# Two transformer blocks on one core: the 256 best keys of query tiles 5 to 7 found by bisection instead of by rounds of eight maxima

## The reference

```python
logits = jnp.einsum('bthd,bsd->bths', qib, k_idx) * (IDX_DIM ** -0.5)
score = jnp.einsum('bth,bths->bts', wb, jax.nn.relu(logits))
score = jnp.where(causal[None], score, -jnp.inf)
_, sel = lax.top_k(score, topk)            # topk = 256
sel_ok = sel <= tb[None, :, None]
k_sel, v_sel = k[sel], v[sel]              # gathered per query
s = jnp.einsum('btkgd,btnkd->btkgn', qg, k_sel) * (HEAD_DIM ** -0.5)
p = jax.nn.softmax(jnp.where(sel_ok, s, -jnp.inf), axis=-1)
o = jnp.einsum('btkgn,btnkd->btkgd', p, v_sel)
```

## Time and profile before

| | |
|---|---|
| median of 3 runs | 2946.56 us (2946.21 to 2955.95) |
| the profiled execution, its own time | 2957.97 us |
| its span, first to last instruction | 2956.2 us |
| mean granted clock of TensorE | 0.97 of full speed |
| busy: PE, DVE, ACT, POOL | 93%, 60%, 23%, 40% of the span |

### The profile page before, as it was taken

How to read it: one execution, slowest core, us unless ns; L and a number is a source line. 1 busy time by engine, 2 the same in 40 slices (tenths; PEclk the granted TensorE clock), 3 DMA queues, 4 the chain that set the end, 5 groups by cost and what they waited for, 6 DMA issues and landing times.

```text
span 2956.2 us, 34504 instructions
## 1 busy us (share of the span) xinstructions
PE 2758.8 (93%) x13488; PEld 2277.8 (77%) x13488; DVE 1763.9 (60%) x2232; ACT 681.4 (23%) x1154; POOL 1196.3 (40%) x791
## 2 busy tenths in 40 slices
PE   4988988999999999999999999788889999999998
PEld 4867766778778888888886768677778888888887
DVE  6288999985566566567566784355535344444335
ACT  4231223443231111000113342122214000111002
POOL 2421476544454344344332323333344344344332
PEclk8999999989999999999999999899999999999999
DMA  6201011110321111111112110000031111111111
GB/s 212 65 12 32 22 58 58 51 43 22 128 72 43 43 57 50 38 54 57 40 50 93 43 36 29 1 1 1 29 129 58 49 57 43 43 57 50 38 54 57
DMA packets 142487, 153.32 MB, mean 52 GB/s; under 512 B 7183, under 2 KB 105252, under 8 KB 142374
## 3 DMA queue, kind: packets, MB, share of 16 engines
q1 hardware_dynamic: 136512, 141.87, 15.2%
q10 hardware_dynamic: 5862, 9.89, 0.9%
HBM read 143.35 MB, written 8.39 MB: 51 GB/s over the span
## 4 chain that ended last, share of the span: by engine, by line
PE 79%; DVE 15%; issue 2%; ACT 2%; POOL 1%; DMA 1%; ACTq 0%; SPq 0%; DVEq 0%; POOLq 0%
PE ps L1813 11%; PE ps L1814 11%; PE ps L1815 11%; PE ps L1798 10%; PE ps L1800 10%; PE ps L1799 10%; PE ps L2200 3%; DVE score L1344 3%; DVE best L1342 3%; DVE yt L1635 2%; PE ps L1972 1%; DVE yt L1624 1%; DVE score L1358 1%; PE ps L1962 1%; PE ps L1998 1%
## 5 line engine op out<-in xcount | busy, mean ns | idle before, releaser
L1798 PE MATMUL ps<-h_hi,w_hi 128*128 128x512 f32 x1472 | 585.3, 398 | 10.3 <-issue 5.6
L1799 PE MATMUL ps<-h_lo,w_hi 128*128 128x512 f32 x1472 | 575.4, 391 | 0.0
L1800 PE MATMUL ps<-h_hi,w_lo 128*128 128x512 f32 x1472 | 575.3, 391 | 0.0
L669 POOL TENSOR_TENSOR w_hi<-raw,zero 128x1024 fp32r<-128x1024 f32 x128 | 243.7, 1904 | 780.3 <-PE ps L1800 397.3
L1813 PE MATMUL ps<-w_hi,u_hi 128*128 128x512 f32 x1024 | 399.2, 390 | 0.0
L1814 PE MATMUL ps<-w_lo,u_hi 128*128 128x512 f32 x1024 | 398.9, 390 | 0.0
L1815 PE MATMUL ps<-w_hi,u_lo 128*128 128x512 f32 x1024 | 398.8, 389 | 0.0
L1519 DVE TENSOR_TENSOR act_r<-act_r 128x512 f32<-128x512 f32 x128 | 167.5, 1309 | 328.9 <-ACT act_r L1035 328.7
L672 POOL TENSOR_TENSOR w_lo<-raw,w_hi 128x1024 fp32r<-128x1024 f32 x128 | 338.1, 2642 | 10.1
L1798 PEld LDWEIGHTS ps<-h_hi,w_hi 128*128 128x128 f32 x1472 | 278.0, 189 | 78.1 <-issue 17.5
L1035 ACT ACTIVATE act_r<-ps 128x512 f32<-128x512 f32 x128 | 76.4, 597 | 1130.8 <-PE ps L1800 1130.8
(11 more groups left out here) (380 smaller groups left out, 4348.4 us busy)
## 6 DMA issues: line engine op xcount, KB each, us to landing
raw<-in_w_up_dram SPq DMA_DIRECT2D x64, 512.0 KB, 4.0
raw<-in_w_down_dram SPq DMA_DIRECT2D x64, 512.0 KB, 3.2
raw<-in_w_ada_dram SPq DMA_DIRECT2D x48, 512.0 KB, 3.7
raw<-in_w_in_dram SPq DMA_DIRECT2D x32, 512.0 KB, 3.7
raw<-in_w_out_dram SPq DMA_DIRECT2D x32, 512.0 KB, 3.2
x<-in_x_dram SPq DMA_DIRECT2D x8, 512.0 KB, 10.8
x<-in_x_dram ACTq DMA_DIRECT2D x8, 512.0 KB, 7.9
x_mid<-x SPq DMA_DIRECT2D x8, 512.0 KB, 5.4
```

The source lines that it names most:

```text
L669: g_.tensor_tensor(w_hi[:, r, :], raw[:, r, :], zero.to_broadcast([P, 1024]), ALU.add).then_inc(sem("w_hi_done"), 1)
L1798: mm(ps[:, bank, :], wh, h_hi[:, k, cols], start=(k == 0), stop=False)
L1799: mm(ps[:, bank, :], wh, h_lo[:, k, cols], start=False, stop=False)
L1800: last = mm(ps[:, bank, :], wl, h_hi[:, k, cols], start=False, stop=(k == NK - 1))
```

## The change

The rounds of tiles 5, 6 and 7 (`SEL_TILES`) are gone. In their place a threshold is found for each of the 3 * 128 queries by bisection over the bits of a float: 1 pass for the sign of the 256th score, 8 for its exponent, 23 for its mantissa, 32 passes (`SEL_PASSES`).

- `sel_pass(k)`, on ACT: three activations, one for each tile (768, 896 and 1024 wide). Each computes the sign of (scale * score + candidate) and sums it along the row into one number. Each waits for the one before it, and pass k waits for step k - 1.
- `sel_step(k)`, on DVE: waits for the three sums, then four linked instructions on 128 x 3 elements accept or refuse the candidates and make the next ones (step 8 has five, the last ten).
- `sel_fin(t, part)`, on DVE: six parts for each tile that correct the last bit, count the keys above the threshold, number the ties by a running sum, keep as many as are wanted, and write the mask.

Passes 0 to 9 stand on ACT between the last scores and the copies `pr_q`; their steps stand on DVE after every third of the rounds 24 to 50, step 9 ahead of the rotation of the queries. Passes 10 to 31 lie in slots 0 to 21, each step in the next slot behind the row maximum. The rounds of tile 4 are spread over slots 0 to 23, and the finishing parts over slots 23 to 29, 32 to 40 and 43 to 48. GpSimd gets five small memsets.

```diff
+SEL_TILES = IDX_TILES[3:]
+NSEL = len(SEL_TILES)
+EXPONENTS = (127, 63, 32, 16, 8, 4, 2, 1)
+SEL_PASSES = 1 + len(EXPONENTS) + 23
...
-        TOPK_SLOTS = {4: range(0, 7), 5: range(7, 20), 6: range(20, 36), 7: range(36, 54)}
+        TOPK_SLOTS = {4: range(0, 24)}
+        SEL_EARLY, SEL_ROUNDS = 10, 3
+        SEL_AT = {k - SEL_EARLY: k for k in range(SEL_EARLY, SEL_PASSES)}
+        FIN_SLOTS = {}
+        for ti, at_slots in zip(SEL_TILES, ((23, 24, 25, 27, 28, 29), (32, 33, 35, 36, 38, 40), (43, 44, 45, 46, 47, 48))):
+            for part, n in enumerate(at_slots):
+                FIN_SLOTS[n] = ("sel_fin", ti, part)
...
                 MICRO.append(("scores", t, i))
+                if n - 1 in SEL_AT:
+                    MICRO.append(("sel_step", SEL_AT[n - 1], 0))
...
+                if n in FIN_SLOTS:
+                    MICRO.append(FIN_SLOTS[n])
+                if n in SEL_AT:
+                    MICRO.append(("sel_pass", SEL_AT[n], 0))
                 if n in ADA_SLOTS:
                     MICRO.append(("ada", ADA_SLOTS[n], 0))
...
+            def sel_pass(k, out):
+                for e, t in enumerate(SEL_TILES):
+                    n = NSEL * k + e
+                    if k == 0:
+                        act.wait_ge(sem("acc_done"), len(INDEX))
+                    else:
+                        act.wait_ge(sem("sel_cand"), k)
+                    if n:
+                        act.wait_ge(sem("sel_sum"), n)
+                    s.activation(out[:, 0:(t + 1) * P], score[t], ACT.Sign, scale=sel_t["sign"][:, e:e + 1] if k else -1.0,
+                                 bias=sel_t["cand"][:, e:e + 1] if k else zero,
+                                 accum_out=sel_t["sum"][:, e:e + 1]).then_inc(sem("sel_sum"), 1)
...
+            for k in range(SEL_EARLY):
+                sel_pass(k, sel_early)
             for t in range(NT):
                 act.wait_ge(sem("tm_full"), 2 * NT + t + 1)
...
+            def sel_step(k):
+                d = sel_t
+                dve.wait_ge(sem("sel_sum"), NSEL * (k + 1))
...
+                link(v.tensor_tensor(d["acc"], d["sum"], d["rank"], ALU.is_le))
+                link(v.tensor_tensor(d["pick"], d["acc"], d["cand"], ALU.mult))
+                link(v.tensor_tensor(d["low"], d["low"], d["pick"], ALU.max))
+                done = len(EXPONENTS)
+                if k < done:
+                    v.tensor_scalar(d["cand"], d["low"], 2.0 ** EXPONENTS[k], None, ALU.mult).then_inc(sem("sel_cand"), 1)
...
+                elif k < SEL_PASSES - 1:
+                    v.scalar_tensor_tensor(d["cand"], d["base"], 2.0 ** (done - 1 - k), d["low"], ALU.mult,
+                                           ALU.add).then_inc(sem("sel_cand"), 1)
...
+            def sel_fin(t, part):
+                e, sc, w = t - SEL_TILES[0], score[t], (t + 1) * P
...
+                junk = sel_out[:, 0:w]
+                if part == 0:
+                    link(v.tensor_scalar(junk, sc, d["sign"], d["pick"], ALU.mult, ALU.is_lt))
+                    link(v.tensor_reduce(d["above"], junk, AX.X, ALU.add))
...
+                if part == 2:
+                    link(v.tensor_scalar(junk, sc, d["kth"], None, ALU.is_gt))
+                    link(v.tensor_reduce(d["higher"], junk, AX.X, ALU.add))
+                    link(v.tensor_scalar(d["ties"], d["higher"], -1.0, float(TOPK), ALU.mult, ALU.add))
+                if part == 3:
+                    link(v.tensor_scalar(junk, sc, d["kth"], None, ALU.is_equal))
+                    link(v.tensor_tensor_scan(junk, ones[:, 0:1].to_broadcast([P, w]), junk, 0.0, ALU.mult, ALU.add))
+                if part == 4:
+                    link(v.tensor_scalar(junk, junk, d["ties"], None, ALU.is_le))
+                    link(v.scalar_tensor_tensor(junk, sc, d["kth"], junk, ALU.is_equal, ALU.mult))
+                if part == 5:
+                    link(v.scalar_tensor_tensor(sc, sc, d["kth"], junk, ALU.is_gt, ALU.add))
+                    link(v.tensor_scalar(sc, sc, 0.0, MASKED, ALU.is_equal, ALU.mult))
...
-            for t, r in ROUND[EARLY_ROUNDS:TOPK_Q]:
+            for n, (t, r) in enumerate(ROUND[EARLY_ROUNDS:TOPK_Q]):
                 topk(t, r)
+                if n % SEL_ROUNDS == SEL_ROUNDS - 1 and n // SEL_ROUNDS < SEL_EARLY:
+                    sel_step(n // SEL_ROUNDS)
```

More of the change, by code:

```diff
@@ L155, in build @@
         alog = small("alog", [P, GH])
+        sel_t = {nm: at(f"sel_{nm}", [P, NSEL], F32, off[0] + 32 * i)
+                 for i, nm in enumerate(("wide", "sum", "rank", "sign", "low", "base", "cand", "acc", "pick", "value", "next",
+                                         "step", "many"))}
+        sel_s = {nm: at(f"sel_{nm}", [P, 1], F32, off[0] + 32 * (13 + i))
+                 for i, nm in enumerate(("above", "is_next", "exact", "kth", "higher", "ties"))}
         abraw = small("abraw", [P, NK, 2 * GH])
@@ L1424, in _ @@
                     topk(t, i)
+                if kind == "sel_step":
+                    sel_step(t)
+                if kind == "sel_fin":
+                    sel_fin(t, i)
                 if kind == "divide":
```

39 lines of the change are left out of this document (added).

## The result

The kernel after takes 2960.84 us (median of 20 runs, 2955.99 to 2964.51), the kernel before 2951.61 us (median of 20 runs beside them, 2946.21 to 2960.27); the ratio is 1.003, with a 95% interval of 1.0021 to 1.0038. That is within the 0.5% that I called no difference, but on the side that I had not forecast: I had said 2940.3.

A forecast was written before the change was run, and what follows sets the result against it. The prediction took PE as the bound over the whole execution and DVE in slots 0 to 47. Its terms, 9.5 + 9 - 24.5 = -6 us, gave 2940.3 us against the median of 2946.6; range 2908 to 2970.

The forecast's parts named there:

- The bound: Attention stage: DVE bounds slots 0 to 21 and 22 to 47 only; slots 48 to 63 gain nothing.
- The early passes, +9.5: Before the attention stage: passes and steps delay the copy of `pr_q` and the queries' rotation; +9.5 us, ends +4 and +14.
- A pass of 3.85 us: ACT: three activations of 1.14 us, each with 0.14 us of waiting for the sum before, 3.85 us a pass.
- A step of 2.3 us: DVE, slots 0 to 21: 0.84 us for four linked instructions plus 1.4 meetings with GpSimd instructions, 2.3 us.
- Slots 0 to 21, +9: First stretch: pass, step and 0.1 us make a slot of 6.25 us, 137.5 us in all; +9, ends -9 and +68.
- That wait is covered, as long as a slot lasts over 5 us: DVE, slots 0 to 21: the next row maximum, done some 8 us after this slot's exponential, is wanted after 12.
- Slots 22 to 47, -24.5: Second stretch: rounds gone, PE needs 143 us, DVE some 102; 153.5 us taken, -24.5, ends -32 and -12.
- The sum: Whole kernel: 9.5 + 9 - 24.5 = -6 us, 2940.3 against the median of 2946.6.
- The loop as the new bound: Rival, slots 0 to 21: steps of 3.45 us, slots of 7.4, stretch +34, sum +19, 2966 us; chance 0.22.
- Steps that run free: Rival: GpSimd mostly idle when steps begin; slots 0 to 21 take 120 us, sum -27, 2920 us; chance 0.30.
- The second stretch that doesn't shrink: Rival, slots 22 to 47: `sel_fin` and GpSimd block each other, only 10 us won, sum +8, 2955 us; chance 0.08.
- ACT is busy for less than 80% of slots 0 to 21 and the stretch is still longer than now: Slots 0 to 21: one of the signs named in advance that would show the forecast wrong.

The follow-up runs named there:

- the pass last: The kernel after with only the order within a slot changed, ScalarE's pass behind the product and the copy of its slot; 2957.22 us, ratio to before 1.0016.
- the kernel without passes: The kernel after with the bisection ended after eleven passes, passes 11 to 31 and their steps left out; 2924.19 us, ratio to before 0.9905.
- the kernel without the loop: The kernel after with attention-stage passes that read a constant column, write unread sums and wait for no step; 2944.60 us, ratio to before 0.9969.
- pointer steps: The kernel after with each step done tile by tile on one column, other operands as per-partition scalars; 2940.26 us, ratio to before 0.9960.
- pointer steps and the pass last: The kernel after with one-column pointer steps in the attention stage, queries' copy after pass 7, and the pass last in its slot; 2930.94 us, ratio 0.9929.
- the shorter execution of the kernel before: Third profiled execution of the unchanged kernel before; 2950.26 us, slots 22 to 47 in 175.11 us.
- The last step alone: The kernel after with only the seven added operations of pass 31's step done tile by tile on one column with pointers; 2957.43 us, ratio to before 1.0010.
- 131.2 in another: The kernel after with four-operation early steps, queries' copy after pass 7, and one-column pointer steps in the attention stage; 2938.73 us, ratio to before 0.9945.

## Why the prediction was wrong

**The bound, right.** DVE held up slots 0 to 47 and nothing behind them: slots 48 to 63 take 101.75 us in every kernel here.

**The early passes, +9.5: right**, though the first profiles of the two kernels seemed to say +6.5. Counted from the last gate copy, which neither kernel moves, they cost 9.5. The mechanism was the one described (passes of 3.9 us, 54.98 us from pass 0 to the copy of `pr_q`, PE idle for 7.4 us where I had said about 5), and moving the copy gives 6.5 of it back.

**A pass of 3.85 us: right**, 3.87 (activations of 1.03, 1.14 and 1.24 us and what stands between them).

**A step of 2.3 us: right** in the mean, 2.13. (The prediction's 1.05 us for the mean GpSimd instruction is 1.10 by its own counts, which would make the step 2.4.)

**Slots 0 to 21, +9: wrong, +16.3 to 16.6.** The step that failed is "a slot of 3.85 + 2.3 + 0.1 = 6.25", and with it "That wait is covered, as long as a slot lasts over 5 us". The sum lets a step begin when its pass ends. From the start of the first pass of the stretch to that of the last there are 140.1 us: 81.1 are the 21 passes, 44.8 the 21 steps, and 13.1 are time in which the pass had ended and the step had not begun, because VectorE was not through with the row maximum that stands ahead of it; 1.1 are left. The sum has nothing for the 13.1. Of these, 12.5 lie in a few places: 2.76 and 2.90 us in the second slots of tiles 1 and 2, 2.94 behind the pass of slot 20, 1.79, 0.92, 0.86 and 0.36 behind four others.

In the second slots of tiles 1 and 2 the attention output of the tile before is split. There VectorE's row maximum stands behind `h_lo`, which waits for `h_hi`, which stands on ScalarE behind the pass and the product. The timeline of ACT and DVE at the first of them:

```profile
417.92 1.24 ACT L950 ACTIVATE sel_out<-score,sel_cand,sel_sign 128x1024 f32<-128x1024 f32 x1
...
419.16 1.13 ACT L1018 ACTIVATE raw<-raw,csil 128x1024 f32<-128x1024 f32 x1
...
420.20 0.57 ACT L1023 ACTIVATE h_hi<-ps 128x512 fp32r<-128x512 f32 x1
...
420.88 0.69 DVE L1553 TENSOR_TENSOR h_lo<-ps,h_hi 128x512 fp32r<-128x512 f32 x1 [3.74 <-ACT h_hi L1023]
```

The exponential then came at 422.13, 8.97 us behind the one before (7.28 us in the kernel before, 6.60 with the pass last). In the kernel with the pass last the late beginnings fall from 13.1 to 2.4 us, but the steps grow by 3.0, and ScalarE, with the product now behind the exponential, is itself late by 3.2 us more, and the first pass begins 1.0 later; 3.7 us of the stretch are won.

In the other places the row maximum waited for PE's scores. Behind the pass of slot 20, PE had waited for GpSimd's diagonal and then worked at the lower level, 0.62 us for a matmul of a tap in place of 0.39:

```profile
489.23 0.56 PE L2115 MATMUL ps<-glu_hi,diag_hi 128*128 128x504 f32 x1 [2.08 <-POOL diag_lo L678]
...
494.56 0.56 DVE L1527 CUSTOM_DVE_ANT_0 prob<-ps,score 128x384 f32<-128x384 f32 x1 [4.38 <-issue]
```

(The profile names no releaser for the second line; PE's last matmul of these scores ends at 494.43.) That slot takes 8.04 us, and 9.13 in the kernel without passes, so this is not the work of the passes. Two more slots are over 8 us, those of 8.24 and 8.06: they hold the two longest steps of the stretch, 4.32 and 4.33 us. PE's waits of 9.4 us for the convolution's bank, behind the copy at L1030, are 6.9 us in the kernel without the loop, 9.0 with pointer steps, and 9.5 with pointer steps and the pass last, so little of the loop's 18.8 us can be theirs. The prediction asked who waits behind the step on DVE, and didn't ask who waits behind the pass on ACT, or whether the step could begin when the pass ended.

**Slots 22 to 47, -24.5: wrong, -19.3** (and -16.6 against the shorter execution of the kernel before). The 153.5 us forecast for this stretch are what it takes when the last step is out of the way (153.20, and 152.79 with pointers); with it, it is 158.5. The step that failed is one that isn't there: the prediction costed "four linked instructions" for every step, though the section on the change says that the last one has ten, seven of them each behind a GpSimd instruction, with slot 23's row maximum behind them. It is the meeting that I had priced, on the longest chain of them, at a place that I didn't ask about. The last step alone is worth 3.8 us; the other 1.2 of the 5 us were not followed.

**The sum.** It was -6 and came to +9. Of the 15 us between, 7.5 are slots 0 to 21, 5 are slots 22 to 47 against the first profile, and 2.7 are in that profile itself, whose second stretch was 177.79 where the third had 175.11. The remaining 5 us between 2940.3 and 2960.8 are the median of the kernel before, 2946.6 of three runs and 2951.6 of twenty.

**The rivals.** The loop as the new bound had the right mechanism and the wrong lever: it asked for steps of 3.45 us, and with steps of 2.13 the kernel was already slower. Steps that run free is what the pointer form makes true: 126.4 us where the rival said 120. There, too, steps begin late, by 9.4 us in all, and neither the rival nor the forecast has that term. The second stretch that doesn't shrink is false. Of the marks in the prediction, "ACT is busy for less than 80% of slots 0 to 21 and the stretch is still longer than now" is the one that came true (79%).

What is still open: why the same attention stage took 126.4 us in one kernel and 131.2 in another. Steps began late by 9.4 and 14.3 us there, the difference lying in slots where the row maximum waited for PE; PE's granted clock was 0.96 and 0.92, and which came first wasn't tried.

## What to carry to other kernels

When work moves from one engine to another, ask of the receiving engine what it did for others and in which order: who stands behind the new work there, in every slot that differs from the usual one. When two engines hand a value back and forth, nearly each us of the shorter side is paid, so bring it into a form that no third engine can hold up, before counting loads. Ask also whether each side can begin when the other ends: a mean for each side leaves that out. And cost the first and the last iteration of a loop by themselves.

## What was unexpected of the hardware

A one-column `tensor_scalar` with two per-partition scalars was never held up by GpSimd (0.28 us in 21 of 21, and 0.64 for three in a row whether GpSimd ran beside them or not), where an instruction with two data operands reached 1.14 us on one column, and one with two such scalars reached 2.30 on three columns. Three of them, at 0.64 us, cost less than a three-column instruction that meets GpSimd (mostly 0.7 to 2.3 us) and more than one that doesn't (0.17 us). When GpSimd had a queue of work, it and VectorE took strict turns: seven instructions of 0.17 us took 8.4 us, one GpSimd instruction for each. And GpSimd didn't pay for it: in slots 0 to 21 it was busy for 89.8 us with steps that met it and 89.6 with steps that didn't.
